# Transposing the mLSTM gate rows from one stacked tile, and spreading the row maxima with one one-pass product

## What is computed

```python
b = jnp.cumsum(jax.nn.log_sigmoid(fc), axis=-1)
m_new = jnp.maximum(b_last + m, g.max(-1))
wk = jnp.exp(g - m_new[..., None])
log_w = jnp.where(causal, b[..., :, None] - b[..., None, :] + ic[..., None, :], -jnp.inf)
inter = b + m[..., None]
m_t = jnp.maximum(inter, log_w.max(-1))
w_prev = jnp.exp(inter - m_t)
s = jnp.einsum('bhtd,bhsd->bhts', qc, kc) * jnp.exp(log_w - m_t[..., None])
num = jnp.einsum('bhts,bhsv->bhtv', s, vc) + w_prev[..., None] * jnp.einsum('bhvk,bhtk->bhtv', C, qc)
h = num / jnp.maximum(jnp.abs(den), jnp.exp(-m_t))[..., None]
```

## Time and profile before

| | us |
|---|---|
| median of 3 runs | 3039.48 (3039.14 to 3041.27) |
| the profiled execution | 3039.09 |
| its span | 3037.3 |
| TensorE busy | 2115.9 (70%) |
| VectorE busy | 2463.1 (81%) |
| ScalarE busy | 888.1 (29%) |

### The profile page before, as it was taken

One profiled execution on the slowest core, in us unless ns is written; L12 is line 12 of the kernel. 1 busy time (PEld: TensorE's weight loads), 2 busy tenths in 40 slices (PEclk: granted clock), 3 DMA queues, 4 the chain that ended last, 5 costly groups with the idle time before them and its releaser, 6 DMA issues.

```text
span 3037.3 us, 24749 instructions
## 1 busy us (share of the span) xinstructions
PE 2115.9 (70%) x8578; PEld 1586.2 (52%) x8578; DVE 2463.1 (81%) x2630; ACT 888.1 (29%) x931; POOL 654.1 (22%) x656
## 2 busy tenths in 40 slices
PE   9999999999999999999999910004656200015653
PEld 7888888888888887888788800001212000002221
DVE  6675688999999887575566899979997899987677
ACT  5544443333334366534455311110000000000001
POOL 0000000000000000000000176773333343333332
PEclk9999999999999999999999955556676655557676
DMA  6454778888988965344354699999999999999997
GB/s 247 173 199 168 296 270 321 330 339 333 337 329 328 343 242 174 145 153 156 125 208 166 223 415 396 418 422 421 421 422 422 422 422 422 422 422 422 421 421 307
DMA packets 133192, 958.53 MB, mean 316 GB/s; under 512 B 14833, under 2 KB 15153, under 8 KB 17137
## 3 DMA queue, kind: packets, MB, share of 16 engines
q0 software_dynamic: 89824, 650.98, 52.7%
q1 hardware_dynamic: 43136, 305.91, 27.4%
q10 hardware_dynamic: 146, 0.53, 0.0%
HBM read 955.23 MB, written 2.13 MB: 315 GB/s over the span
## 4 chain that ended last, share of the span: by engine, by line
PE 57%; DMA 25%; DVE 13%; issue 3%; POOL 2%; ACT 1%; SPq 0%; POOLq 0%; DVEq 0%; ACTq 0%
DMA rows_g<-in_v_tab_dram,idx 18%; PE bank L647 17%; PE bank L651 17%; PE bank L648 17%; DVE rows_g L2677 8%; DMA rows_g<-in_u_tab_dram,idx 6%; PE bank L1190 2%; POOL rows_g L621 2%; PE bank L681 1%; DVE bank L2726 1%; PE bank L1004 0%; DMA raw<-in_wstream_dram 0%; PE bank L950 0%; PE bank L689 0%; PE bank L860 0%
## 5 line engine op out<-in xcount | busy, mean ns | idle before, releaser
L1815 DVE TENSOR_TENSOR WL<-raw,WH 128x2048 fp32r<-128x2048 f32 x287 | 657.1, 2291 | 290.7 <-ACT WH L1204 284.8
L1190 PE MATMUL bank<-rows_g,diag 128*128 128x512 f32 x488 | 363.9, 915 | 725.2 <-DMA rows_g<-in_v_tab_dram,idx 725.2
L647 PE MATMUL bank<-WH,UH 128*128 128x512 f32 x1952 | 770.4, 395 | 3.3 <-DVE WL L1815 2.9
L651 PE MATMUL bank<-WH,UL 128*128 128x512 f32 x1952 | 761.1, 390 | 0.0
L648 PE MATMUL bank<-WL,UH 128*128 128x512 f32 x1952 | 760.3, 389 | 0.0
L1204 ACT ACTIVATE WH<-raw 128x2048 fp32r<-128x2048 f32 x287 | 550.3, 1918 | 679.3 <-DMA raw<-in_wstream_dram 665.8
L1190 PEld LDWEIGHTS bank<-rows_g,diag 128*128 128x128 f32 x488 | 139.2, 299 | 950.7 <-issue 660.3
L2677 DVE CUSTOM_DVE_ANT_0 rows_g<-rows_g,bank 128x2048 f32<-128x2048 f32 x233 | 524.8, 2285 | 36.6 <-DMA rows_g<-in_u_tab_dram,idx 36.0
L2726 DVE SCALAR_TENSOR_TENSOR bank<-rows_g,gate_w,bank 128x2048 f32<-128x2048 f32 x193 | 454.5, 2355 | 116.5 <-DMA rows_g<-in_v_tab_dram,idx 98.1
L647 PEld LDWEIGHTS bank<-WH,UH 128*128 128x128 f32 x1952 | 367.0, 188 | 79.6 <-issue 2.6
L651 PEld LDWEIGHTS bank<-WH,UL 128*128 128x128 f32 x1952 | 366.7, 188 | 76.9
(11 more groups left out here) (409 smaller groups left out, 1618.2 us busy)
## 6 DMA issues: line engine op xcount, KB each, us to landing
raw<-in_wstream_dram SPq DMA_DIRECT2D x288, 1024.0 KB, 4.9
ada_w<-in_ada_dram POOLq DMA_DIRECT2D x96, 1024.0 KB, 7.5
rows_g<-in_u_tab_dram,idx POOLq DMA_INDIRECT x256, 24.0
rows_g<-in_v_tab_dram,idx POOLq DMA_INDIRECT x256, 30.1
X<-in_x_dram SPq DMA_DIRECT2D x4, 512.0 KB, 9.9
c_row<-in_c_rows_dram POOLq DMA_DIRECT2D x1, 2048.0 KB, 8.6
ctx_x<-in_ctx_dram POOLq DMA_DIRECT2D x1, 2048.0 KB, 10.4
gb<-mod_rows POOLq DMA_DIRECT2D x2, 1024.0 KB, 5.6
```

What stands on the lines that cost most here:

```text
L647: pe.matmul(o, ah[:, k0 + k, t], wh[:, w], start=first and k == 0, stop=False)
L651: mm = pe.matmul(o, al[:, k0 + k, t], wh[:, w], start=False, stop=last and k == nk - 1)
L1190: mm = pe.matmul(bank[c], diag[:, n % 2, :], row(q)[:, c * CW:(c + 1) * CW], start=s == mine[0], stop=s == mine[-1])
L1815: dve.tensor_tensor(WL[:, n % SLOTS_W, :], raw[:, n % SLOTS_W, :], WH[:, n % SLOTS_W, :].bitcast(F32), ALU.subtract).then_inc(lo_ready, 1)
```

## The change

The latents' rows A, wk, exp(..M) and ex are put on partitions 0, 32, 64 and 96 of one tile, `l_stack` (A and wk are views of it, ScalarE writes the other two there). It lies where A lay, and is cleared ahead. `columns` turns all four kinds by one product of 100 rows and 16 columns for each direction and chunk; its moving operand is the identity, columns 0 to 3 of each 32. The latents' columns all stand behind step 21, with nothing of them behind step 22. The context's columns are as before.

The row maxima go into `l_far`, 36 partitions of type fp32r: -M rounded on partitions 0 to 3 and what the rounding left on 32 to 35, the rest zero. `begin` multiplies them by `far_hot` (two stacked identities, 36 x 4, one column repeated 128 times) in one one-pass product. It reads the 128 columns twice, 256 in all; the second half falls on columns that L1004 begins anew. VectorE gets three instructions at the start of `gate_rows` for the latents (the sum for `far_hot`, the clearing of `l_stack`, the copy of its zeros to `l_far`) and one more at its end.

```diff
@@ -445,6 +445,11 @@
         l_rows = [view(f"l_row{i}", "P", o, [2, T])[0:MH, :, :]
                   for i, o in enumerate((NB * O_G, H_VM + CW, O_G + H_O + CW, NB * O_G + CW, H_O + CW, O_G + H_U))]
 
+        l_stack = view("l_stack", "P", NB * O_G, [2, T])
+        l_far = view("l_far", "P", O_G + H_O + CW, [2, T], F32R)
+        far_hot = tiny("far_hot", [MH], F32R)
+        LO, STACKED, FAR = 32, 3 * 32 + MH, 32 + MH
+
         class Stream:
 
 
@@ -465,7 +470,8 @@
                     self.k_raw = lambda n, b: P2[:, n, H_K + b * P:H_K + (b + 1) * P]
                     self.k_tok = lambda n, o, w: P2[:, n, H_VM + o:H_VM + o + w]
                     self.v = lambda n: P2[:, n, H_VM:H_VM + D_ML]
-                    self.A, self.lf, self.b, self.M, self.wk, self.ex = l_rows
+                    _, self.lf, self.b, self.M, _, self.ex = l_rows
+                    self.A, self.wk = l_stack[0:MH, :, :], l_stack[LO:LO + MH, :, :]
                 self.steps = [(step, d, step if d == 0 else NB - 1 - step) for step in range(NB) for d in range(2)]
 
         streams = [Stream(0), Stream(1)]
@@ -916,19 +922,18 @@
                         mm = pe.transpose(banks[j][:, m * P:(m + 1) * P], S.kT(4 * (j % 2) + m)[:, span(j // 2)], ident[:, :])
                     mm.then_inc(sem("k_back"), 1)
 
-            def columns(S, part=None):
+            def columns(S):
 
                 pe.wait_ge(sem("rows_ready"), S.s + 1)
-                kinds = [S.A, S.wk, S.lf, S.ex] if S.lat else [None, S.wk]
-                for kind, row in enumerate(kinds):
-                    if row is None or (part is not None and kind // 2 != part):
-                        continue
-                    for d in range(2):
-                        for n in range(NB):
-                            o = ((kind * 2 + d) * NB + n) * MH
-                            pe.matmul(DB[2][:, o:o + MH], row[:, d, span(n)], ident[0:MH, 0:MH], start=True, stop=True)
-                if part == 0:
-                    return
+                for d in range(2):
+                    for n in range(NB):
+                        if S.lat:
+                            kinds = DB[2][:, 0:4 * 2 * NB * MH].rearrange("p (k d n h) -> p k d n h", k=4, d=2, n=NB)
+                            pe.matmul(kinds[:, :, d, n, :], l_stack[0:STACKED, d, span(n)],
+                                      ident[0:STACKED, :].rearrange("p (k c) -> p k c", c=32)[:, :, 0:MH], start=True, stop=True)
+                        else:
+                            o = ((2 + d) * NB + n) * MH
+                            pe.matmul(DB[2][:, o:o + MH], S.wk[:, d, span(n)], ident[0:MH, 0:MH], start=True, stop=True)
                 for d in range(2):
                     for n in range(NB):
                         o = ((4 * 2 + d) * NB + n) * MH
@@ -998,7 +1003,8 @@
                     pe.wait_ge(sem("h_ready"), x - 3)
                 elif x >= 2:
                     pe.wait_ge(sem("state_ready"), ML_UNITS + min(x - 1, ML_UPDATES))
-                pe.matmul(e[:, 0:P], ident[0:MH, h:h + 1].to_broadcast([MH, P]), L.b[:, d, span(n)], start=True, stop=False)
+                pe.matmul(e[:, 0:2 * P].rearrange("p (r t) -> p r t", r=2), far_hot[0:FAR, h:h + 1].to_broadcast([FAR, P]),
+                          l_far[0:FAR, d, span(n)].unsqueeze(1).to_broadcast([FAR, 2, P]), start=True, stop=False)
                 pe.matmul(e[:, 0:P], ident_b[:, :], mask_b[:, d, :], start=False, stop=True)
                 for kt in range(MKT):
                     mm = pe.matmul(e[:, P:P + VA], qT(MKT * h + kt)[:, span(n)], st[:, d, h, kt, :],
@@ -1066,9 +1072,8 @@
                 turn(lambda j, m: P2[:, m % 2, H_Q + (2 * j + m // 2) * P:H_Q + (2 * j + m // 2 + 1) * P], DB, "q_turned")
                 yield from until(21)
                 pe.wait_ge(sem("q_pad_ready"), 4)
-                columns(L, 0)
+                columns(L)
                 yield from until(22)
-                columns(L, 1)
                 yield from until(25)
                 pe.wait_ge(sem("co_ready"), 2)
                 keys_back(L, DB)
@@ -1513,14 +1518,13 @@
                 act.wait_ge(sem("rows_made"), 2 * S.s + 2)
                 for d in range(2):
                     for n in range(NB):
-                        seq.mark(act.activation(S.wk[:, d, span(n)], S.A[:, d, span(n)], ACT.Exp,
-                                                  bias=n_ml[0:MH, d, n:n + 1]))
+                        seq.mark(act.activation(S.wk[:, d, span(n)], S.A[:, d, span(n)], ACT.Exp, bias=n_ml[0:MH, d, n:n + 1]))
                 seq.mark(act.activation(dcy[0:MH, :, :], dcy[0:MH, :, :], ACT.Exp))
                 if S.lat:
                     for step, d, n in S.steps:
-                        seq.mark(act.activation(S.lf[:, d, span(n)], S.M[:, d, span(n)], ACT.Exp, scale=-1.0,
+                        seq.mark(act.activation(l_stack[64:64 + MH, d, span(n)], S.M[:, d, span(n)], ACT.Exp, scale=-1.0,
                                                   bias=m_st[0:MH, d, NB + step:NB + step + 1]))
-                    seq.mark(act.activation(S.ex, S.ex, ACT.Exp, scale=-1.0))
+                    seq.mark(act.activation(l_stack[96:96 + MH, :, :], S.ex, ACT.Exp, scale=-1.0))
                 seq.sync()
                 act.sem_inc(sem("rows_acted"), 1)
 
@@ -2239,6 +2243,10 @@
 
             def gate_rows(S):
                 dve.wait_ge(sem("gate_ps"), 2 * S.s + 2)
+                if S.lat:
+                    link.mark(dve.tensor_tensor(far_hot[0:FAR, :], ident[0:FAR, 0:MH], ident[0:FAR, LO:LO + MH], ALU.add))
+                    link(dve.memset(l_stack[0:STACKED, :, :], 0.0))
+                    link(dve.tensor_copy(l_far[0:FAR, :, :], l_stack[0:FAR, :, :]))
                 for typ, dst in ((0, S.A), (1, S.lf)):
                     for d in range(2):
                         link.mark(dve.tensor_scalar(dst[:, d, :], DB[2 + typ][0:MH, d * T:(d + 1) * T],
@@ -2274,7 +2282,8 @@
                     link(dve.tensor_tensor(S.ex, S.b, S.M, ALU.add))
                 dve.sem_inc(sem("rows_made"), 1)
                 if S.lat:
-                    link(dve.tensor_scalar(S.b, S.M, -1.0, None, ALU.mult))
+                    link(dve.tensor_scalar(l_far[0:MH, :, :], S.M, -1.0, None, ALU.mult))
+                    link(dve.scalar_tensor_tensor(l_far[LO:LO + MH, :, :], S.M, -1.0, l_far[0:MH, :, :], ALU.mult, ALU.subtract))
 
             def rows_done(S):
                 dve.wait_ge(sem("rows_acted"), 2 * S.s + 2)
```

## The result

The kernel after takes 3034.18 us, the median of 20 runs (3030.75 to 3038.89). The kernel before, timed beside it, takes 3039.33 us (20 runs, 3035.54 to 3043.64). The ratio is 0.9982 with a 95% interval of 0.9976 to 0.9988. That is 5.15 us less by the medians, 5.5 by the ratio (3.6 to 7.3 by its interval). The prediction was 3034.8 us, a gain of 4.7 us. The change (0.18%) is smaller than the 0.2% that the prediction takes for the least that can be told apart; the interval lies clear of 1 all the same.

The account below looks back on a forecast made before the run. TensorE's instruction stream was taken as the bound, so savings pass on one to one: 2.95 + 1.76 = 4.7 us off the median of 3039.48 gives 3034.8 us, with an 8-in-10 range of 3029.8 to 3038.5.

Parts of the forecast that it names:

- Part 1: Latents' gate-row transposes (columns): one break of 16 instructions replaces two breaks costing 5.13 us, saving 2.95 us.
- Part 2: Row maxima spread in begin, 16 times: one one-pass product replaces a full-precision pair, saving 0.11 us each, 1.76 us.
- Do the losses stay at 36 rows?: Around begin's new product: the 0.31 us lost going in and out stays, as with 4 and 32 rows; chance 0.52.
- VectorE costs nothing: Added VectorE work for the latents, at most 1.7 us, delays the weight split at most 0.2 us; TensorE doesn't wait.
- What follows starts earlier and takes as long: After the projection stage: output projection, queries and gathers start earlier, unchanged in length; the saving passes on one to one.
- Rival 1: In begin: 36 rows count as full height, saving 0.33 to 0.39 us each time; 3031.0 us, at best 3030.3; chance 0.27.
- Rivals 2 and 3: In begin: precision change costs 0.5 us, 3036.1 (0.10, including one clock fall); product not one full-pace pass, 3041.1 us (0.05).
- Rival 5: At the first columns break: the change doesn't do what it says, rows_ready comes late and TensorE stands; adds nothing.
- Rival 4: Clock falls behind the new columns break (1.8 us, 3036.6) or in begin (all 13: 3058 us); several falls, chance 0.04.

Follow-up runs that it names:

- the part alone: Kernel before with only the latents' rows stacked and turned by one product, row maxima spread as before: stretch 292.15 us against 295.26, ratio 0.9987.
- the heights: Kernel after with the one-pass product reading 36, 64, 68 and 128 rows for heads 0 to 3, added rows zero: stretch 288.41 us against 290.63.
- the two repeats of before: Kernel before, unchanged, profiled twice more on the last kernel's chip: stretches 298.48 and 298.46 us against 295.26 in its first profile.
- Full height in before: Kernel before with the full-precision pair that spreads the row maxima reading 128 rows instead of 4, added rows zero: stretch 293.75 us, ratio 0.9981.
- part 2 alone: Kernel after with the latents' columns in two breaks as before, keeping the one-pass product of 36 rows: stretch 296.92 us, ratio 0.9993 of before.
- The width: Kernel after with the one-pass product writing its 128 columns once instead of twice: stretch 289.59 us, 1.04 us less than after's.

## Why the prediction was right, and where not

**The sum held, term by term, for the profile it was made against.** Forecast 4.7 us, found 4.63 in the stretch.

- *Part 1*, forecast 2.95, found 3.10 (5.13 - 2.03); the part alone gave 3.11. The break costs less than the 2.12 to 2.21 us I took because it loses nothing going in: 100 rows follow 128 without a step. I had carried over the old break's full 0.31 us. The step inside, from 100 rows to 4, is the 0.08 us that I had allowed for.
- *Part 2*, forecast 1.76, found 1.5. The steps are the predicted ones: 0.10 going in and 0.31 after, 0.11 us less. But in the first eight units 0.03 us of that is lost in the chunk products behind, so 8 x 0.08 + 8 x 0.11 = 1.5 us.
- *Do the losses stay at 36 rows?* Yes. This was the open choice, 0.52 to 0.27, and the heights decide it for the forecast: 1.27 us with 36 rows and 1.28 with 64, against 1.00 with 68. It was in part luck. Of the two rows of loss that the choice rested on, that of 32 rows has 4 weight columns and keeps its loss at 128 rows, so it says nothing of the height that 36 was set beside; only the row of 4 rows bears on it. The Trainium skill (TensorEngine Tiling, sections Available Configurations and Key Properties) has modes of 32, 64 and 128 rows and a drain when the mode changes; the boundary between 64 and 68 rows agrees with it. Here the price is 0.28 us for going in and out together.
- *VectorE costs nothing.* Right, and the slack is 5 us or more. The split still waits for ScalarE, 0.18 us of the old 1.46. It starts 0.48 us later than in before, no more than the 0.57 by which the whole stretch is later. The copy took 0.42 us, under the 0.68 bound.
- *What follows starts earlier and takes as long*: 1476.3 us against 1476.6.

**The rivals.** Rival 1 fell with the heights; its best case stands there as 3030.3 us, and as 3029.8 at the end of the range. Rivals 2 and 3 fell with the unit: its step of 0.31 us holds 0.11 for the product and the same 0.20 as before, so it is one pass at full pace with nothing added for the change of precision. Rival 5 fell with the two rows that changed as drawn.

**Rival 4 had the right mechanism on the wrong side.** I priced a fall of the clock behind a break of small instructions at 1.8 us and asked whether the *new* break would have one. The evidence that the old ones had none was a single profile. Four further executions with those breaks all have two falls, which cost some 3.2 us in each of the two repeats of before (298.47 - 295.26). The merged break has none in nine. So the change also takes away a cost that I hadn't seen.

Whole executions point the same way. Full height in before gains 1.5 us in the stretch against the first profile, but 5.8 us (3.0 to 8.5) by its ratio to timed executions of before. That fits if most of those had the falls too. How much of the measured 5.5 us comes from that can't be read from the runs; that the total came out at the forecast is partly luck. With falls in four of five executions it would be 0.8 x 3.2 = 2.6 us beside the 4.6, 7.2 in all, at the edge of the interval (3.6 to 7.3). The falls may be rarer than five profiles say. Ahead of the stretch something may also be given back: in after the clock is 0.79 at 1216 to 1224 us, and in before it is 0.79 at 1248 to 1256, 8 x 0.21 = 1.7 us in either place. The first of these falls is in four of the nine profiles with the merged break and in none of the five with two.

**What stays open.** The context's own break of columns, with the same instructions in both kernels, has a fall at 1248 to 1256 us in before, in both repeats and in full height in before, not in part 2 alone, and in none of the nine with the merged break. TensorE's instructions ahead of it are the same, and I have no explanation that a run supports. Why the first profile of before kept its clock at 1384 us isn't known either.

**The expectations that missed** by more than a few tenths have two causes. Part 2 alone and full height in before were each some 3 us too slow in the stretch, both by falls of the clock, while their units did as said. The width missed because neither of its two cases let the product shrink.

## What to carry over

Between full-height products, a TensorE product of 4, 36 or 64 rows cost about 0.3 us beyond its columns here, 16 times in one stage; filling it with zero rows to 68 or 128 removes that. It costs one clearing on a VectorE that has the slack and at 128 rows took 4.65 us more off the stretch, as much as the whole change. Merging two short breaks into one gained 3.1 us, by 24 fewer instructions and fewer steps between heights, and no fall of the clock was seen behind the merged one. Before a stretch's clock enters a sum as a fact, look at it in more than one profiled execution: the one I had was the exception among five.

## What the hardware showed that I had not expected

- A one-pass product's cost round full-height work has two values: 1.27 to 1.28 us a unit at 36 and 64 rows, 0.99 to 1.00 at 68 and 128.
- Full-precision products with 4 weight columns lose the same 0.31 us at 128 rows as at 32 (2.47 us either way).
- 128 columns in one pass take about 0.06 us less than 256; no lower limit of time shows at this size.
- Behind each of two breaks of 16 and 24 instructions of 4 rows, one chunk apart, the granted clock fell to 0.50 for some products in four of five executions (0.79 to 0.99 over rows of 8 us). Behind one break of 16, at least half of them of 100 or 128 rows, it did so in none of nine.
- The best kernel here is full height everywhere with the narrow product: 3026.02 us, 0.9956 (0.9942 to 0.9969) of before, against 0.9982 for the change.
